# Decode keys turned by VectorE in 32 by 32 blocks, and logits contracted over 32 rows in sixteen tiles of the array

## The reference, cut to what matters

```python
D_MODEL, SEQ, DEC_BATCH, DEC_SEQ, PAST_LEN, PAGE_SIZE = 1024, 512, 8, 8, 2048, 128
B_HEADS, B_DH = 8, 64
...
def attend_selected(q, kg, vg, valid):
    logits = jnp.einsum('bthd,btkhd->bhtk', q, kg) * (B_DH ** -0.5)
    logits = jnp.where(valid[:, None], logits, -jnp.inf)
    p = jax.nn.softmax(logits, axis=-1)
    return jnp.einsum('bhtk,btkhd->bthd', p, vg)
```

## Time and profile before

| | us |
|---|---|
| median of 3 runs | 763.51 (761.39 to 763.83) |
| the profiled execution | 759.38 |
| its span | 757.7 |
| the decode loop in it | about 260 to 533 |
| PE busy, in the span | 717.0 (95%) |
| DVE busy | 464.5 (61%) |
| ACT busy | 245.0 (32%) |
| POOL busy | 202.2 (27%) |

### The profile page before, as it was taken

The page is one execution under the profiler, slowest core; times in us unless marked ns, Lnnn a source line. Parts: engine busy times, 40 slices in busy tenths (PEclk is TensorE's granted clock), DMA queues, the critical chain, the costliest instruction groups (busy, mean ns, idle before and its releaser), DMA issues.

```text
span 757.7 us, 13976 instructions
## 1 busy us (share of the span) xinstructions
PE 717.0 (95%) x4842; PEld 413.8 (55%) x4842; DVE 464.5 (61%) x976; ACT 245.0 (32%) x559; POOL 202.2 (27%) x329
## 2 busy tenths in 40 slices
PE   4987999999999999999999999999999999879994
PEld 3534444444544555677665556777456677754441
DVE  0204279999999865554556555554747676674435
ACT  3203720114667422222222323222743335430000
POOL 1550005015798722222222222222000002650000
PEclk9989999999999999999999999999999999989998
DMA  9930052042130088898887889886200007400611
GB/s 228 293 109 1 2 204 104 34 146 83 62 113 1 29 266 254 284 351 275 262 277 259 254 255 329 294 270 185 82 1 2 1 2 279 112 15 24 198 42 42
DMA packets 60949, 114.12 MB, mean 151 GB/s; under 512 B 8241, under 2 KB 21634, under 8 KB 60882
## 3 DMA queue, kind: packets, MB, share of 16 engines
q1 hardware_dynamic: 29890, 50.37, 21.1%
q0 software_dynamic: 12512, 40.34, 16.2%
q10 hardware_dynamic: 18480, 22.55, 9.1%
HBM read 106.01 MB, written 7.23 MB: 149 GB/s over the span
## 4 chain that ended last, share of the span: by engine, by line
PE 85%; DVE 3%; DMA 3%; ACT 2%; issue 2%; another core or an unknown queue 2%; ACTq 1%; POOL 1%; SPq 0%; DVEq 0%; POOLq 0%
PE banks L547 16%; PE banks L807 12%; PE banks L793 8%; PE banks L721 7%; PE banks L1072 7%; PE banks L769 4%; PE banks L738 4%; PE banks L895 3%; PE banks L882 3%; PE banks L913 2%; PE banks L685 2%; PE banks L758 2%; PE banks L631 2%; DMA arena<-in_x_prompt 2%
## 5 line engine op out<-in xcount | busy, mean ns | idle before, releaser
L547 PE MATMUL banks<-wbuf,xT 128*128 128x512 f32 (+1 forms) x448 | 150.1, 531 | 3.4 <-issue 3.4
L336 POOL DMA_DIRECT2D arena<-in_cache_v x128 | 68.9, 539 | 198.7 <-issue 198.7
L547 PEld LDWEIGHTS banks<-wbuf,xT 128*128 128x128 f32 (+1 forms) x448 | 66.8, 175 | 80.8 <-issue 74.9
L807 PE MATMUL banks<-wbuf,xT 128*128 128x512 f32 (+1 forms) x288 | 105.0, 530 | 0.0
L1526 DVE TENSOR_REDUCE small<-banks 128x1 f32<-128x512 f32 x32 | 22.1, 691 | 93.0 <-PE banks L738 93.0
L1507 DVE MAX8 small<-arena 64x8 f32<-64x2112 f32 x32 | 75.2, 2348 | 1.3
L1509 DVE MATCH_REPLACE8 arena<-small,arena 64x2112 f32<-64x2112 f32 x32 | 74.7, 2334 | 0.0
L721 PE MATMUL banks<-ident,arena 128*128 128x128 f32 x512 | 68.1, 276 | 0.2 <-DMA arena<-in_cache_k 0.2
L721 PEld LDWEIGHTS banks<-ident,arena 128*128 128x128 f32 x512 | 56.4, 141 | 21.6 <-issue 19.8
L793 PE MATMUL banks<-xT,arena 128*128 128x288 f32 x256 | 67.4, 406 | 0.0
L1270 ACT COPY wbuf<-banks 128x512 f32<-128x512 f32 x64 | 37.2, 582 | 70.0 <-PE banks L721 70.0
(11 more groups left out here) (250 smaller groups left out, 1031.0 us busy)
## 6 DMA issues: line engine op xcount, KB each, us to landing
arena<-in_cache_k SPq DMA_DIRECT2D x128, 256.0 KB, 3.4
arena<-in_cache_v POOLq DMA_DIRECT2D x128, 256.0 KB, 3.9
wbuf<-in_w_in ACTq DMA_DIRECT2D x8, 2048.0 KB, 11.3
arena<-in_w_in ACTq DMA_DIRECT2D x8, 512.0 KB, 6.3
arena<-in_x_prompt SPq DMA_DIRECT2D x4, 512.0 KB, 4.7
wbuf<-in_w_out SPq DMA_DIRECT2D x1, 2048.0 KB, 8.0
xT<-in_w_out SPq DMA_DIRECT2D x1, 2048.0 KB, 13.1
out<-wbuf SPq DMA_DIRECT2D x1, 2048.0 KB, 9.4
```

The source lines that it names most:

```text
L336: e.dma_start(buf[n % 2][:, i, :], cache[bass.ds(pg, 1), 0].rearrange("a p h d -> p (a h d)")).then_inc(arrived[n % 2], 16)
L547: mm = pe.matmul(psum[a * NS:a * NS + ROWS[t], n % PB, 0:w // split], xT[:, c, t * P:t * P + ROWS[t]], wbuf[:, WB[g], c, a * w // split:(a ...
L807: mm = pe.matmul(psum[a * NS:a * NS + ROWS[t], bank, 0:512 // split], xT[:, c, t * P:t * P + ROWS[t]], wbuf[:, WB[g], c, a * 512 // split: ...
```

## The change

`turn_keys` leaves PE. DVE turns each step's keys from `k_buf` into `kg` with two instructions of 128x1024, each of which turns every 32 by 32 block by itself. After that a column block 4j + e of `kg`, in rows 32a to 32a + 31, holds a quarter e of the pair of heads j, for the keys 32a to 32a + 31 of every page. So `logits(n)` contracts over 32 rows: for each quarter e, each row group a and each pair j one matmul of 128 columns with 16 weight columns, 64 matmuls (128 records) in place of 4 (8 records). The four row groups write to four banks, `LB` to `LB + 3`; all of them are used in every step, so `logits(n)` now waits for `exponential(n-1)` instead of `exponential(n-2)`. The mask is added by four matmuls of 128 columns, one for each bank, and these stand ahead of the wait for the turned keys. `logits_new` works in the same way on two row groups (2 mask matmuls and 32 matmuls of 32 columns in place of 1 and 4), with keys turned once by DVE, and writes behind the scores in banks `LB` and `LB + 1`; at g = 3 `negmax` and `exponential` wait for it too, and ACT's `exponential` for the maximum of both.

The copies of turned keys (`keys_out`) go away on both engines; `probs_out` moves from DVE to ACT. The queries are stacked in SBUF by eight small DMAs (`qst`), turned once by DVE (`q32`), and set out for each sequence by ACT into one of two buffers that POOL cleared early. In `gather_out`'s step DVE now does both halves of the turning first, then `gather_out`, then two `strike`s. SP asks for the pages of step n when DVE has turned those of step n - 2 (`kg_ok`). PE's transposes of the new keys and new queries go away, and ACT copies all four prompt query tiles out, where DVE did two.

```diff
-                def turn_keys(n, half):
-
-                    if half == 0:
-                        pe.wait_ge(k_in[n % 2], 64 * (n // 2) + 64)
-                    for j in (2 * half, 2 * half + 1):
-                        pe.wait_ge((kg_dve, kg_act)[j % 2], 2 * n + j // 2)
-                        for i in range(4):
-                            mm = pe.transpose(psum[:, KB0 + j % 2, i * P:(i + 1) * P],
-                                              k_buf[n % 2][:, i, j * P:(j + 1) * P], ident[:])
-                        mm.then_inc(kg_tr, 1)
...
                 def logits(n):
                     s, g = n // 4, n % 4
-                    pe.wait_ge(kg_dve, 2 * n + 2)
-                    pe.wait_ge(kg_act, 2 * n + 2)
-                    if n >= 2:
-                        pe.wait_ge(ex, q_no(n - 2) + 1)
-                    bank = psum[:, SB0 + n % 2, :]
-                    pe.matmul(bank, pick[:, s * P:(s + 1) * P], bias_s[:, g * 512:(g + 1) * 512], start=True, stop=False,
-                              skip_group_check=True)
-                    for j in range(4):
-                        mm = pe.matmul(bank[32 * j:32 * j + 32, :], queries(s, j), kg[n % 2][:, j, :],
-                                       start=False, stop=(j == 3), skip_group_check=True)
+                    if n:
+                        pe.wait_ge(ex, q_no(n - 1) + 1 + (g == 0))
+                    if g == 0:
+                        pe.wait_ge(qbd_ok, 2 * s + 2)
+                    masks = bias_s[:, g * 512:(g + 1) * 512].rearrange("p (i a c) -> p a i c", i=4, a=4)
+                    for a in (2, 3, 0, 1):
+                        pe.matmul(psum[:, LB + a, 0:P], pick[:, s * P:(s + 1) * P], masks[:, a], start=True, stop=False,
+                                  skip_group_check=True)
+                    pe.wait_ge(kg_ok, 2 * n + 2)
+                    for e in range(4):
+                        for a in range(4):
+                            r = slice(32 * a, 32 * a + 32)
+                            for j in range(4):
+                                mm = pe.matmul(psum[32 * j:32 * j + 16, LB + a, 0:P], qbd_v[s % 2][r, j, e],
+                                               kg_v[n % 2][r, :, 4 * j + e, :], start=False, stop=(e == 3),
+                                               skip_group_check=True)
                     mm.then_inc(qk, 1)
...
+                def turn_keys(n, half):
+                    if half == 0:
+                        dve.wait_ge(k_in[n % 2], 64 * (n // 2) + 64)
+                        if n >= 2:
+                            dve.wait_ge(qk, q_no(n - 2) + 1)
+                    w = slice(1024 * half, 1024 * half + 1024)
+                    nc.vector.transpose(kg[n % 2][:, w], k_buf[n % 2].rearrange("p g n -> p (g n)")[:, w]).then_inc(kg_ok, 1)
```

203 lines of the change are left out of this document (105 added, 98 removed).

## The result

The changed kernel takes **791.41 us** (median of 4 runs, 789.14 to 792.88) against 763.67 us (761.39 to 763.97) for the kernel before, a ratio of 1.0367 with an interval of 1.0331 to 1.0403. It is slower by 27.7 us; the forecast was 740.4, faster by 23.1, and the measured time lies outside the range of 724 to 772. The profiled execution took 792.68 us, its span is 791.0.

What follows compares the result with a forecast made beforehand. The prediction took PE to bound the decode loop. Its terms, -45.4 + 9.8 + 1.5 + 2.4 + 5.6 + 3 = -23.1 us, took 763.5 to 740.4 us, range 724 to 772.

Steps and rivals of the forecast that it cites:

- Masks: PE, each decode step: four masks of 128 columns instead of one of 512, taken as 0.4 us, at most 1.2.
- Logits: PE, each decode step: 128 short records on 16 overlapping array parts, 1.0 us plus 0.1 and 0.2 for layout changes.
- the 12 named as the sign of failure: PE's logits: weight loads of L742 more than 12 ns apart would show the prediction wrong.
- the first rival: PE's logits: array parts don't overlap beyond four, 3.3 us instead of 1.0; 820 us, slower; chance 0.14.
- The last rival: PE's records: issue slower than in a burst, 11 ns a record, 17 us back, 757 us; chance 0.09.
- Turning by DVE: DVE, each decode step: turning 1024 columns takes 1.14 us, 2.3 a step, covered by PE's other work.
- the slow-turning rival: DVE turns keys at half the pace, 4.6 us a step; 769 us, slower by under 1%; chance 0.08.
- Waits for `gather_out`: PE at the values, seven steps: waits for DVE of 1.65 us (three) and 1.2 us (four), 9.8 us in all.
- Hand-over of the exponential: PE's turning of probabilities: exponential late, 1.5 us over about 15 steps, plus 2.4 us in 8 steps behind `logits_new`.
- `logits_new`: PE, new keys' logits in 8 steps: about 1.1 us against 0.4 before, 5.6 us in all.
- Transfers: Decode loop's DMA: share 0.91 in a loop of some 250 us, local lateness likely, 3 us.
- a rival of 751: Decode loop: transfers bind at a share of 0.87, loop lasts 261 us, 12 us gained; chance 0.12.

Runs made afterwards that it cites:

- e9: Changed kernel with `gather_out` moved on DVE from behind the next step's turnings to behind `shares`: 769.37 us, 1.0214 to the kernel before.
- e4: Changed kernel with half of the logits' contraction left out (64 records a step instead of 128): 719.92 us, 0.959 to the kernel before.
- e1: Changed kernel with each decode-loop page load fetching one row instead of 128 from step 2 on: 760.61 us, 1.0103 to the kernel before.
- e12: Changed kernel with the logits' 128 records over 64 columns instead of 128: 784.16 us, 1.0402 to the kernel before.
- e3: Kernel before with 54 extra matmuls of 8 columns (108 records) a step behind the values: 787.88 us, 1.0459 to the kernel before.
- e2: Kernel before with each decode-loop page load fetching one row from step 2 on: 751.64 us, 0.9986 to the unedited kernel before.
- e7: Changed kernel with the cached keys' logits as 16 matmuls of 128 rows by 64 columns instead of 64 matmuls: 745.18 us, 0.9879 to the kernel before.
- e6: Changed kernel with the logits' loops over row parts and column parts swapped: 772.82 us, 1.0286 to the kernel before.
- e10: Kernel before with 108 extra matmuls of 8 columns a step in one block behind the values: 950.13 us, 1.2593 to the kernel before.
- e13: Changed kernel with two steps' logits at once, 128 records over 256 columns every second step, and `gather_out` behind `shares`: 751.34 us, 0.9953 to the kernel before.
- e14: e13 with the new keys' logits moved behind the turned probabilities of the step before: 735.02 us, 0.9658 to the kernel before.
- e8: Changed kernel with each step's logits cut in two and a quarter of the next unit between: 784.24 us, 1.0423 to the kernel before.
- e15: e14 with the pair's logits cut in two and a quarter of the unit between: 734.82 us, 0.9661 to the kernel before.

## Why the prediction was wrong

What bounds the kernel, the steps before and what PE loses were read rightly. Of its own terms, in the order of the prediction:

- **Masks**: taken as 0.4, measured 437.64 - 437.31 = 0.33. Right.
- **Logits, 1.0 plus 0.2 to change back** (and 0.1 ahead): measured 1.78. This is the term of PE's sum that was mis-sized, by 0.5 us a step, some 16 us over the 31 steps from the first mask to the last. The prediction took the larger of two bounds, 0.84 for the columns and 0.95 for the handing over at 7.4 ns, as if the smaller hid behind the larger. The runs show that a fixed price and the columns add. With 64, 128 and 256 columns the group takes 1.35, 1.78 and 2.64 us: each further column costs a record 0.0525 ns, which times 16 parts is 0.84 ns, about one part's own price for a column (105 ns for 128, by the prediction's rows). So the columns of sixteen parts do overlap in full. What is left at no columns, 0.92 us, is 0.2 for the change of layout and 0.72 for 128 records, 5.6 ns each. The 7.4 ns came from the weight loads of a burst of eight. The same row had 89 ns, 12.7 each, between the starts of its eight matmuls, and the prediction passed over that. Here the matmuls start 12.5 ns apart in the mean ((1.85 - 0.27) / 127), but most of the first 32 only 7 ns apart, with holes of 85 and 109 ns behind them: a burst of eight could not show it. The weight loads stand 11.6 ns apart, just under the 12 named as the sign of failure. In all the group costs (1.78 - 1.3) / 128 = 3.8 ns more a record than was taken, less than the 5.0 from which the first rival decides for slower.
- **Instruction supply**: not in the prediction at all, put at nothing without a reason, and the larger part. The last rival, "the issue is slower than in a burst", came nearest, but as a pace of 11 ns and not as stops. 15 stops of 30.3 us, some 29 of them over and above the usual gap.
- **Clock**: the prediction took it as full. Half clock for 37.5 us can cost at most half of that, 19 us. Counted record by record against the same pairs of records at full clock, the stretches at 1.2 GHz cost an estimated 11 us.
- **Turning by DVE**, 1.14 estimated, 1.217 measured; PE never waited for the keys. Right, and the slow-turning rival falls. The Trainium skill ("Vector Engine (DVE) Microarchitecture Reference", 3.8) says that this turning sustains one element a cycle and lane; the trace agrees in so far as 1.19 ns a column is close to the 1.11 of the plain DVE row, with no second pass over the data.
- **Waits for `gather_out`**, 9.8 forecast: 7.3 in six waits, the longest 1.7 for 1.65 forecast, and e9 took them away again. Right in mechanism and about in size; that one of them has half clock behind it was not foreseen.
- **Hand-over of the exponential**, 1.5 + 2.4 = 3.9 forecast: nothing on PE. Only the weight loads wait there:

```profile
PEld banks L764 <- ACT arena L1284: 7.2, 13, 0.7
```

The matmuls of L764 start as soon behind the unit's last record as they did before (0.43 us with 512 columns), and no wait of PE at L764 stands in the view above.
- **`logits_new`**, 0.7 more a time: the changed kernel has a stop in each of these steps, so the size is read from e4, which has the same new keys' logits and masks. There such a step takes 7.66 against 6.36 us, 1.30 more, where the kernel before had 8.79 against 8.08, 0.71 more. That is 0.6 a time. Right.
- **Transfers**, 3 us and a rival of 751: a share of 0.76, no wait for a page. They did cost, but in another way than thought: e1 shows that they delay the packets of instructions.
- The rule of the Trainium skill ("TensorE: Matmul & The Clock Gate", "Wait — 56ns, not 53.3ns?") that starts of matmuls never come closer than about 25 ns, by which the prediction reckoned 818 us, does not hold here on different parts of the array: 12.5 ns in the mean, 9.5 with 64 columns (e12) and 8.7 on four parts with 8 columns (e3). The time came out between the forecast and that rival, for another reason than either.

Sum for the loop, first to last mask: forecast 241.1 us. 16 more for the logits and 29 for stops, 2.5 less for `gather_out`, 3.9 for the hand-over and 3 for the transfers make 276.7, and the trace has 292.7. Of the 16 left over, about 11 are the clock by the count above; 5 stay without a name. The other 5 us of the profiled executions' difference lie outside. 3.8 of them are a loop that starts later, 270.5 against 266.8; in e1 and e4, with the same code ahead of it, it starts at 257.0 and 255.2, earlier than in e2 and e3 on that chip (259.1, 259.2). So they are not of the change.

Two steps failed, then. The smaller is "I take 1.0 us", the larger bound where both add: 1.78 us measured for 1.3, 0.5 us a step. By itself it would have left the change faster, as steps of 7.18 us for 8.08 show and e7's 0.988 bears out. What turned the sign is the step that the prediction left out. It asked for each new matmul how long PE needs, and of the 4608 new records never how their instructions reach PE, though the page of before had the queue that brings them: 15 stops, some 29 us, and the half clock behind them.

Left open: what makes the 5.6 ns a record and the holes behind the first 32 (order, e6, does not); when a packet is asked for, since only its transfer is in the records; and why the clock falls behind some stops and not behind others of the same length. A layout of 64 rows by 32 columns, with half the records again, would need its own maximum for half of the rows and was not tried.

## What to carry to other kernels

When a change trades few long instructions for many short ones, count the instructions that stand in a row and divide by the time they take. Here 256 in under about 3 us mostly made PE stop, for up to 4.7 us in the changed kernel (13 of 16 blocks there, 30 of 35 in e10), at times with the clock down behind it, while no block of the kernel before, at 10 us and more, ended in a stop. What helped was fewer instructions with more columns in each (pairs of steps, e13) and moving work out of the burst (e14); a burst made shorter in time alone made the kernel no faster (e12), and long work put into it gained nothing by itself (e8, e15). And for a pace on many array parts, add the fixed price to the columns instead of taking the larger.

## What the runs showed of the hardware

- PE's instructions come in packets of 16 KB, 256 instructions with the matmuls' weight loads counted. At the stops of all runs a packet takes 0.9 to 2.2 us, and PE goes on 1.2 to 1.7 us behind its end. Its start behind PE's entry into a block varies: the median is 0.9 us with light transfers (e1), 1.8 in the changed kernel and 3.1 to 3.2 in the pairs kernels (e13 to e15).
- In e10 blocks of 256 that end in a stop take 4.1 us in the median and once 1.9, otherwise at least 3.0, from entry to entry; a few pass in 1.4 to 1.9 us without a stop.
- Page loads at 250 GB/s lengthen the wait for such a packet by delaying its start, by 0.9 us in the median of the stops (e1 against the changed kernel).
- fp32 matmuls of 32 rows by 16 columns on 16 parts of the array take, in a group of 128 records, 5.6 ns plus 0.0525 ns a column (64, 128 and 256 columns); at 128 columns the order of the parts makes no difference (e6).
- In the changed kernel six of 15 stops, of 1.8 to 4.7 us, have 3.4 or 6.8 us at 1.2 GHz that begin in them or up to 1.9 us behind, and nine have none. A record of 512 columns then takes 0.85 instead of 0.43 us. e7, with no stops, had 6.8 us of it, behind two of its waits for `gather_out`.
